# A two-layer decoder trunk on one core: the later modulation pieces issued from GpSimd's queue instead of SyncE's

## The reference

```python
c_act = silu(c)
for layer in (0, 1):
    shift_t, scale_t, gate_t, shift_m, scale_m, gate_m = split(c_act @ ada_w[layer] + ada_b[layer], 6)
    h = rms_norm(x) * (1 + scale_t) + shift_t
    y = dilated-window attention (layer 0: three groups of q, k, v; then w_o)
        or differential attention (layer 1: q from h; k, v from x with a modulation of their own; then w_o)
    x = x + gate_t * y
    h = rms_norm(x) * (1 + scale_m) + shift_m
    x = x + gate_m * (relu(h @ w1) ** 2 @ w2)
```

## Time and profile before

| | |
|---|---|
| median of three runs | 2492.49 us |
| the profiled execution | 2487.57 us |
| its span, first to last instruction | 2485.8 us |
| TensorE, VectorE, ScalarE, GpSimd busy | 97%, 72%, 50%, 2% |
| transfers on SyncE's queue | 663.46 MB, 73.3% of the 16 DMA engines' time |
| TensorE's granted clock, mean | 0.992 of full speed |

### The profile page before, as it was taken

How to read it: one execution, slowest core, us unless ns; L and a number is a source line. 1 busy time by engine, 2 the same in 40 slices (tenths; PEclk the granted TensorE clock), 3 DMA queues, 4 the chain that set the end, 5 groups by cost and what they waited for, 6 DMA issues and landing times.

```text
span 2485.8 us, 28422 instructions
## 1 busy us (share of the span) xinstructions
PE 2417.1 (97%) x11121; PEld 1997.6 (80%) x11121; DVE 1801.4 (72%) x2164; ACT 1237.4 (50%) x2046; POOL 49.0 (2%) x82
## 2 busy tenths in 40 slices
PE   5999999999999999999999999999999999999999
PEld 5787888887788888888887887878788888888887
DVE  7768787877878787778787796777785545445554
ACT  3355555555543443543545675654653453443442
POOL 2000000000000000000001000000100000000000
PEclk9899999999999999999999999999999999999999
DMA  8878787874979888878896886656795555555555
GB/s 344 342 263 308 292 314 279 335 258 178 378 287 355 313 325 293 329 284 331 289 346 219 322 319 223 251 212 228 285 348 179 189 184 195 187 186 191 189 186 169
DMA packets 150485, 665.27 MB, mean 268 GB/s; under 512 B 16880, under 2 KB 17360, under 8 KB 120912
## 3 DMA queue, kind: packets, MB, share of 16 engines
q1 hardware_dynamic: 150352, 663.46, 73.3%
HBM read 661.30 MB, written 2.10 MB: 267 GB/s over the span
## 4 chain that ended last, share of the span: by engine, by line
PE 76%; DVE 11%; ACT 6%; DMA 3%; issue 3%; SPq 0%; DVEq 0%; ACTq 0%
PE main L384 22%; PE main L382 22%; PE main L383 22%; DVE w_lo L1204 3%; DVE acc L1218 3%; ACT w_hi L847 2%; PE main L396 2%; PE main L398 2%; PE main L397 2%; DMA qT<-ada 2%; PE tr L467 1%; DVE acc L1235 1%; DMA w_raw<-w 1%; ACT st_a L887 1%; ACT st_b L873 1%
## 5 line engine op out<-in xcount | busy, mean ns | idle before, releaser
L847 ACT ACTIVATE w_hi<-w_raw 128x1024 fp32r<-128x1024 f32 x800 | 841.5, 1058 | 926.6 <-DMA w_raw<-w 922.4
L1204 DVE TENSOR_TENSOR w_lo<-w_raw,w_hi 128x1024 fp32r<-128x1024 f32 x800 | 968.5, 1223 | 418.7 <-ACT w_hi L847 415.2
L382 PE MATMUL main<-w_hi,hT_hi 128*128 128x512 f32 x1840 | 732.6, 398 | 1.1 <-ACTq L891 1.1
L384 PE MATMUL main<-w_hi,hT_lo 128*128 128x512 f32 x1840 | 717.9, 390 | 0.0
L383 PE MATMUL main<-w_lo,hT_hi 128*128 128x512 f32 x1840 | 717.0, 390 | 0.0
L1218 DVE SCALAR_TENSOR_TENSOR acc<-ada_raw,c_act,acc 128x2048 f32<-128x2048 f32 x165 | 387.6, 2349 | 50.6 <-DMA ada_raw<-ada 50.0
L384 PEld LDWEIGHTS main<-w_hi,hT_lo 128*128 128x128 f32 x1840 | 345.5, 188 | 73.0
L382 PEld LDWEIGHTS main<-w_hi,hT_hi 128*128 128x128 f32 x1840 | 345.9, 188 | 71.7 <-issue 1.7
L383 PEld LDWEIGHTS main<-w_lo,hT_hi 128*128 128x128 f32 x1840 | 346.1, 188 | 70.2 <-issue 1.2
L382 PE MATMUL main<-w_hi,mid_hi 128*128 128x512 f32 x960 | 377.7, 393 | 0.0
L384 PE MATMUL main<-w_hi,mid_lo 128*128 128x512 f32 x960 | 377.2, 393 | 0.0
(11 more groups left out here) (234 smaller groups left out, 1783.4 us busy)
## 6 DMA issues: line engine op xcount, KB each, us to landing
w_raw<-w SPq DMA_DIRECT2D x800, 512.0 KB, 4.0
ada_raw<-ada SPq DMA_DIRECT2D x208, 1024.0 KB, 6.8
qT<-ada SPq DMA_DIRECT2D x16, 1024.0 KB, 7.5
gate<-bias_rows SPq DMA_DIRECT2D x4, 1024.0 KB, 7.5
xs<-x SPq DMA_DIRECT2D x1, 2048.0 KB, 7.9
out<-xs SPq DMA_DIRECT2D x3, 512.0 KB, 5.8
out<-xs SPq DMA_DIRECT2D x2, 256.0 KB, 2.5
st_a<-lamb SPq DMA_DIRECT2D x1, 256.0 KB, 9.3
```

Source lines behind the costliest of these rows:

```text
L382: pe.matmul(acc_ps[:, :], hi[:, kt, tc], w_hi[:, s, wc], start=(kt == 0), stop=False)
L384: last = pe.matmul(acc_ps[:, :], lo[:, kt, tc], w_hi[:, s, wc], start=False, stop=(kt == PK * pairs - 1))
L847: act.activation(w_hi[:, s, :], w_raw[:, s, :], ACT.Copy).then_inc(hi_done, 1)
L1204: dve.tensor_tensor(w_lo[:, s, :], w_raw[:, s, :], w_hi[:, s, :].bitcast(F32), ALU.subtract).then_inc(lo_done, 1)
```

## The change

SyncE's program loses `ada_piece` and all tables; after the opening it issues weights, biases and outputs alone, so a weight piece now waits for `mm_done` only. GpSimd's program gains `ada_pieces(count)`: for each of `count` pieces it waits for `ada_used`, as SyncE did, and issues the transfer from its own queue. It has five calls of it, between its staging steps: after the opening, 48 pieces; after the two pairs before the output projection, 6; after the first change of sub-layer, 92; after the second, 32; after the third, 14. Buffers, places of use on VectorE, the pieces and their order stay as they are.

```diff
             def weight_piece():
...
-            def ada_piece():
-                n["ada"].up()
-                s = (n["ada"].n - 1) % ADA_SLOTS
-                if n["ada"].n == 2 * KT + 1:
-                    sp.wait_ge(ada_mm, 2 * KT)
-                sp.wait_ge(ada_used, n["ada"].n)
-                sp.dma_start(ada_raw[:, s, :], av[n["ada"].n - 1]).then_inc(ada_in[s], 16)
...
-            def chunk(ch, pieces=PIECES, ada=()):
-                for j in range(pieces):
+            def chunks(count, pieces=PIECES):
+                for _ in range(count * pieces):
                     weight_piece()
-                    if (ch, j) in ada:
-                        ada_piece()
...
-                    chunk((g, c), ada=ADA_QKV)
-
-            for ch in range(4):
-                chunk(ch, PIECES // 2, after((2, 3)) + ADA_WO)
...
+                    chunks(1)
+            chunks(4, PIECES // 2)
+            chunks(1)
             bias(1, 4)
...
+            def ada_pieces(count):
+                for _ in range(count):
+                    n["ada"].up()
+                    s = (n["ada"].n - 1) % ADA_SLOTS
+                    pool.wait_ge(ada_used, n["ada"].n)
+                    pool.dma_start(ada_raw[:, s, :], av[n["ada"].n - 1]).then_inc(ada_in[s], 16)
...
             stage(range(PIECES), x_rows)
+            pool.wait_ge(ada_mm, 2 * KT)
+            n["ada"].up(2 * KT)
+            ada_pieces(len(ADA_QKV))
 
             pool.wait_ge(den_inv, 1)
             stage(range(2), head_rows)
             n["hT"].up(2)
+            ada_pieces(DRAIN + len(ADA_WO) + len(ADA_ENTRY))
...
             arrive(2)
+            ada_pieces(len(ADA_GATE) + len(ADA_FIRST) + len(ADA_MLP) + ADA_SLOTS)
             arrive(4)
+            ada_pieces(len(ADA_Q) + len(ADA_V) + len(ADA_ENTRY) - ADA_SLOTS)
             n["hT"].up(PIECES)
             arrive(6)
+            ada_pieces(len(ADA_GATE_B))
```

More of the change, by code:

```diff
@@ L307, in _ @@
                     first_ada(FIRST_PIECES * j + a)
-            n["ada"].up(2 * KT)
             sp.dma_start(gain_rot[:, :, :].rearrange("p g e -> p (g e)"),
@@ L317, in _ @@
                         bias(0, 0)
-                    chunk((g, c), ada=ADA_QKV)
-            for ch in range(4):
-                chunk(ch, PIECES // 2, after((2, 3)) + ADA_WO)
-            chunk(0, ada=ADA_ENTRY)
+                    chunks(1)
+            chunks(4, PIECES // 2)
+            chunks(1)
             bias(1, 4)
[L325 to L330, removed]
-            bias(2, 4 + 16)
[L332 to L336, removed]
-            bias(3, 4 + 16 + 4)
[L338 to L344, removed]
+            chunks(8 + 8 + 8 + 7 + 1)
+            bias(2, 4 + 16)
+            chunks(3 + 12 + 1)
+            bias(3, 4 + 16 + 4)
+            chunks(8 + 8 + 8 + 7)
             rows = out.rearrange("(t p) d -> p t d", p=P)
```

## The result

The changed kernel takes 2518.51 us, the median of four runs (2513.09 to 2520.20), against 2491.80 for the kernel before in the same runs: 1.0123 times, 95% interval 1.0108 to 1.0139. The forecast was 2490 with a range up to 2508. The profiled execution has a span of 2516.4 us, 30.6 more than before.

A forecast was written before the change was run, and what follows sets the result against it. TensorE was taken as the bound, VectorE setting its pace in places. Terms -3.2 + 0 + 0.8 + 0 = -2.4 took 2487.6 to 2485.2; 4.9 up to the median gave 2490, range 2480 to 2508.

The forecast's parts named there:

- What bounds the kernel: Whole span: TensorE is the bound, lacking 10.4 us in short windows; SyncE's holds are mostly a symptom of late VectorE.
- The 3.2 us of gain in the sum: SyncE's waits and 192 issues go: 1.3 us gained at 210 to 250, 1.1 at 1320, 0.8 at 1430.
- the pieces are issued earlier: Third step: pieces go once their buffer is free; +0.8 us at the end of the opening, price 0 elsewhere.
- The 5 us of cover: Slack for a late weight piece, reckoned from 860 to 1320 us: 16.4 us per slot round, less the work, leaves 5.
- The earlier trace at 640 to 660: With DMA engines at 0.99 and 387 GB/s there, TensorE lacks nothing; given in support of price 0.
- GpSimd's issues: 192 waits and issues added between GpSimd's staging steps: 0.98 us each, nothing on the path waits, price 0.
- VectorE beside it: VectorE while GpSimd builds transfers: 0 taken; 15 us if 80 pieces cost 0.19 each, 78 if fully blocked.
- rival B: GpSimd's transfer work stretches VectorE's instructions from 155 to 540 and 1370 to 1750 us: 15 us, 2508; chance 0.18.
- The end of the opening: Two modulation pieces, 2 MB, go beside the weight transfer of 152.44: +0.8 us, up to +3.2.
- Rival C: Two queues serve weights worse from 620 to 860 us, 5% of the rate lost: 7 us, 2500; chance 0.12.

The follow-up runs named there:

- e1: Changed kernel, but GpSimd issues each modulation piece not before mm_done allows its table entry's weight piece, as SyncE did: 1.0028 times the kernel before.
- e9: e1 with each modulation piece allowed one weight piece earlier, ada_used still binding: 1.0033 times the kernel before.
- e8: Kernel before, all issues on SyncE, with each of the 192 modulation pieces issued one weight piece later than in the table: 1.0078 times the kernel before.
- e3: Changed kernel with each of the 192 modulation transfers cut to 256 of 2048 columns, issues and waits kept: 2482.96 us, 0.9985 times the kernel before.
- e4: Kernel before with the 192 modulation transfers cut to 256 of 2048 columns, still issued by SyncE: 2482.75 us, 0.9979 times the kernel before.
- e5: Changed kernel with only the first two modulation pieces after the opening kept at the old moment of issue: 2515.41 us, 1.0111 times the kernel before.
- e13: Kernel before, with ten semaphore increments and waits on SyncE (about 1 us) between each modulation piece's buffer wait and issue: 1.0019 times the kernel before.
- e12: e9 with five small chained memsets on GpSimd before each modulation issue, a delay of 1.0 us: 1.0068 times the kernel before.
- e11: e1 with five small chained memsets on GpSimd before each modulation issue, a delay of 1.0 us: 1.0083 times the kernel before.
- e10: e1 with each modulation piece allowed two weight pieces earlier, the moment often set by VectorE's buffer release: 1.0065 times the kernel before.
- e6: Changed kernel with the old moments of issue for only the first 48 modulation pieces (layer 0's queries, keys and values): 1.0057 times the kernel before.
- e2: Changed kernel with each modulation piece issued as two transfers of 128x1024, rows of 4 KB instead of 8: 2524.56 us, 1.0147 times the kernel before.

## Why the prediction was wrong

- **What bounds the kernel** was right: TensorE, with VectorE near its limit from 155 us on. That taking the holds away wins nothing fits all runs (e1, e9 and the changed kernel have none, e8 has 31 us), though in each of them something else changed too. The 3.2 us of gain in the sum can't be found in any run that moves all bytes.
- **The step that failed** is the third, "the pieces are issued earlier", with its sentence "a weight piece meets a modulation piece beside it instead of ahead of it" and its "Price 0". Measured, the queue with the old moments costs 0.28% (e1), 7 us, some of it from e1's own held staging; letting the moments go costs the other 0.95%, 24 us (the changed kernel against e1).
- **Why the sum missed it.** The 5 us of cover were worked out in the first MLP, where TensorE lacks nothing, and there they hold: no loss from 860 to 1320 in either kernel. They were then used for the stage from 155 to 540, where the changed kernel loses 19.8 us. That ScalarE's and VectorE's side work takes the cover there, so that one late piece is handed on, is read from the chain at 242.32 and from ScalarE's 58% against 45%; no run took that work away. VectorE's share, by which the prediction told the stages apart, is the same in both. The earlier trace rows at 640 to 660 answered for a stage that has slack.
- **GpSimd's issues** cost nothing, as said; the row is 0.53 us instead of 0.98. **VectorE beside it** (rival B, whose 2508 came nearest in time) was wrong as a mechanism: the splits stay at a median of 1224 ns, L1189 at a mean of 2345, and e3 equals e4. The rule weighed there, of the Trainium skill (SBUF — State Buffer, the warning on VectorE blocking DMA), that GpSimd can't write descriptors while VectorE runs a double-rate instruction, shows in no run: the changed kernel's 192 issues take 0.53 to 0.73 us each on GpSimd.
- **The end of the opening** was sized at +0.8 with +3.2 as the far end. The weight piece took 6.88 us, and TensorE's stop before 164 us grew from 1.05 to 4.38, so +3.3; but e5 shows that little of it reaches the end.
- **Rival C** came nearest as a mechanism, weights that land later, with the wrong place and form: a lost rate from 620 to 860. The first MLP lost 4.7 us in all; the rate there is as good as before (335 GB/s from 620 to 860, 331 in the changed kernel from 641 to 881), and single pieces came late elsewhere. That it takes two queues isn't so either: in e13 they land as late on one, at a price of 0.2%.

How the 1.2% divide: at most 0.3 for the queue, 0.35 to 0.55 for being out of phase (e12 against e9, e11 against e1), and a rest of 0.4 to 0.6. The rest is a difference, not an experiment, and it is mostly the 19.8 us of the stage to 540. There the changed kernel's pieces are released at VectorE's pace alone. e10, with pieces at most two weight pieces early, loses 5.3 us there, and e6, with the old moments, 4.5. So the moments of issue are the cause; what in them makes the larger part, how far ahead the pieces go or how irregularly, no run separates.

Why a wrong phase costs 0.2% on one queue (e13) and 0.35 to 0.55 on two, at about the same median landing, is not settled. A second hardware queue, on ScalarE, was not tried, since its waits would have stopped ScalarE's own work.

No kernel here beats the one before. With seven eighths of the traffic worth 0.2% (e4), there was hardly room.

## What to carry to other kernels

A hold in an issuing queue is worth removing only if the engine it waits for isn't itself the late one; look at that engine's timeline beside the hold first. A stream of transfers that shares a queue with the critical one also gets its timing from it: move it, and its moments come loose, so keep them tied (here by the same semaphore as the weights) and test the queue and the moments apart. An added wait on an in-order engine also holds what is queued behind it, as in e1: look at its other work before the run is read as a clean test. Take the cover for a late transfer from the stage in which it will be late, not from the one with the cleanest numbers.

## What the runs showed of the hardware that was not expected

- A 1 MB transfer of 128 rows takes GpSimd 0.53 us to issue (192 issues, mean 531 ns), and at the same moments it lands no later than from SyncE: 6.4 us against 6.7 (e1 and before, 155 to 560 us).
- Moving such transfers by about 1 us against a stream of 512 KB every 2.7 us raised the stream's median landing from 4.3 to 5.0 (e9, e12) or 5.3 us (e1, e11), and from 4.4 to 5.3 on one queue (before, e13), all from 155 to 560 us.
- Halving the rows of one queue's transfers from 8 to 4 KB gave the other queue nothing: 5.4 us instead of 5.0 (e2 and the changed kernel).
